# Logits ahead of transposes in two attentions, and one exponential moved behind a rounding copy

## What is computed

```python
def fox_prompt(q, k, v, logf):            # first attention, 8 heads x 64, causal
    s = jnp.einsum('bqhd,bshd->bhqs', qb, k).astype(jnp.float32) * scale
    s = s + cq[..., None] - ct[:, :, None, :]
    s = jnp.where(kpos[None, :] <= qpos[:, None], s, -jnp.inf)
    p = jax.nn.softmax(s, axis=-1).astype(v.dtype)
    return jnp.einsum('bhqs,bshd->bqhd', p, v)

def dsa_select_attend(...):               # second attention, 8 query heads on 2 key heads
    score = jnp.where(adm[None], score, -jnp.inf)
    _, idx = lax.top_k(score, top_k)      # the kernel adds a mask made of the scores instead
    return gathered_attention(q, k, v, idx, valid)
```

## Time and profile before

| | |
|---|---|
| median of 3 runs | 1360.31 us (1359.1 to 1361.63) |
| the profiled execution | 1360.25 us, span 1358.5 us |
| TensorE busy | 1317.5 us, 97% of the span |
| VectorE busy | 954.9 us, 70% |
| ScalarE busy | 676.5 us, 50% |
| first attention | about 296 to 427 us of the span |
| second attention | about 431 to 562 us of the span |

### The profile page before, as it was taken

The page is one execution under the profiler, slowest core; times in us unless marked ns, Lnnn a source line. Parts: engine busy times, 40 slices in busy tenths (PEclk is TensorE's granted clock), DMA queues, the critical chain, the costliest instruction groups (busy, mean ns, idle before and its releaser), DMA issues.

```text
span 1358.5 us, 23643 instructions
## 1 busy us (share of the span) xinstructions
PE 1317.5 (97%) x8868; PEld 1179.8 (87%) x8868; DVE 954.9 (70%) x1795; ACT 676.5 (50%) x1250; POOL 541.6 (40%) x518
## 2 busy tenths in 40 slices
PE   7989999989999999999999999999999999999997
PEld 7859999977877777778899999999999997678886
DVE  4399989898886989767855654555654556576497
ACT  5479979838885888510443222233223333343330
POOL 3406684532322132335645555555555452000011
PEclk9999999999999999999999999999999999999999
DMA  7102432259784622511045435445434459787452
GB/s 248 55 16 63 158 110 78 71 139 213 183 214 102 151 51 63 195 47 63 16 140 179 151 114 165 139 147 179 144 121 157 138 195 345 259 284 247 171 189 106
DMA packets 150369, 197.17 MB, mean 145 GB/s; under 512 B 28120, under 2 KB 106872, under 8 KB 150256
## 3 DMA queue, kind: packets, MB, share of 16 engines
q1 hardware_dynamic: 150256, 195.67, 46.6%
HBM read 136.69 MB, written 48.38 MB: 136 GB/s over the span
## 4 chain that ended last, share of the span: by engine, by line
PE 52%; DVE 3%; DMA 1%; issue 1%; ACT 1%; POOL 0%; POOLq 0%; SPq 0%; DVEq 0%; ACTq 0%
PE banks L2886 32%; PE banks L2258 6%; PE banks L2984 4%; PE banks L2985 4%; PE banks L2986 4%; DMA down_raw<-in_w_down 1%; DVE rows L3372 1%; DVE down_lo L3240 0%; PE banks L2860 0%; PE banks L3002 0%; DVE h_B_lo L3275 0%; DVE h_T_lo L3275 0%; PE banks L2356 0%; PE banks L2354 0%; ACT down_hi L3138 0%
## 5 line engine op out<-in xcount | busy, mean ns | idle before, releaser
L3160 POOL TENSOR_TENSOR w_lo<-w_S,w_hi 128x512 fp32r<-128x512 f32 x88 | 119.2, 1354 | 110.0 <-ACT w_hi L3039 110.0
L2886 PE MATMUL banks<-h_T_hi,w_hi 128*128 128x264 f32 x704 | 144.6, 285 | 0.2 <-DVE h_T_lo L3275 0.2
L2886 PE MATMUL banks<-h_T_lo,w_hi 128*128 128x264 f32 x704 | 143.7, 285 | 0.0
L2886 PE MATMUL banks<-h_T_hi,w_lo 128*128 128x264 f32 x704 | 142.9, 283 | 0.0
L3138 ACT CAST down_hi<-down_raw 128x1024 fp32r<-128x1024 f32 x77 | 80.7, 1051 | 123.8 <-PE banks L2986 62.1
L3039 ACT CAST w_hi<-w_S 128x512 fp32r<-128x512 f32 x88 | 54.7, 622 | 167.3 <-PE banks L2886 147.4
L2230 POOL TENSOR_TENSOR ln_rstd<-ln_var_eps,ln_power 128x1 f32<-128x1 f32 (+1 forms) x18 | 25.1, 1393 | 255.8 <-DVE ln_var_eps L2221 136.8
L3240 DVE TENSOR_TENSOR down_lo<-down_raw,down_hi 128x1024 fp32r<-128x1024 f32 x77 | 93.0, 1228 | 45.7 <-ACT down_hi L3138 45.5
L2984 PE MATMUL banks<-down_hi 128*128 128x512 f32 x308 | 121.0, 393 | 1.5 <-DVE rows L3372 1.1
L2986 PE MATMUL banks<-down_hi,down_lo 128*128 128x512 f32 x308 | 120.5, 391 | 0.0
L2985 PE MATMUL banks<-down_lo,down_hi 128*128 128x512 f32 x308 | 120.4, 391 | 0.0
(11 more groups left out here) (424 smaller groups left out, 3779.5 us busy)
## 6 DMA issues: line engine op xcount, KB each, us to landing
down_raw<-down_a SPq DMA_DIRECT2D x77, 256.0 KB, 4.0
gate_raw<-in_w_gate SPq DMA_DIRECT2D x11, 1024.0 KB, 6.5
down_t<-in_w_down SPq DMA_DIRECT2D x44, 256.0 KB, 4.1
down_w<-down_t SPq DMA_DIRECT2D x22, 512.0 KB, 3.4
down_raw<-in_w_down SPq DMA_DIRECT2D x22, 512.0 KB, 6.8
down_raw<-down_w SPq DMA_DIRECT2D x44, 256.0 KB, 4.3
up_raw<-in_w_up SPq DMA_DIRECT2D x10, 1024.0 KB, 6.3
down_a<-down_s SPq DMA_DIRECT2D x10, 1024.0 KB, 4.1
```

The lines of the kernel that those rows point to most:

```text
L2886: mm = nc.tensor.matmul(pp[:, bank[to] + ch, 0:PIECE], l, x[name][:, k, ch * PIECE:(ch + 1) * PIECE], start=opens and k == 0 and i == 0, s ...
L3160: nc.gpsimd.tensor_tensor(w_lo[n % 2][:, :, :], weight(m, SCHEME[q][0]), f32(w_hi[n % 2][:, :, :]), ALU.subtract).then_inc(w_lo_done, 1)
```

## The change

TensorE takes the first of a slot's logits ahead of the slot's transposes and the others behind them. This holds in both attentions, where the slot has a step and this is not one of a sample. The wait for banks and parts still stands ahead of both. Nothing is added or removed: the same instructions stand in another order.

On ScalarE, in the first attention alone (`own_first=True`), a slot with the first step of a batch now takes ahead of the rounding copy only those waiting exponentials that belong to that batch; the others come behind it.

```diff
--- before.py
+++ after.py
@@ -1321,7 +1321,7 @@
 def attention(nc, ctx, pl, exps, scales, c, tag, batches, parts_of_steps, ahead, source, loads, pe_first, act_first, dve_first, logits, bias,
               sample_values, sample_cols, places, out_sample, sp_beside=None, act_beside=None, pool_beside=None,
               dve_beside=None, pe_beside=None, pe_between=None, act_between=None, dve_between=None, spread=False, idle=(0, 0, 0), scales_soon=2 * NT,
-              sums_in_logits=False, pe_last=None, banks=None):
+              sums_in_logits=False, pe_last=None, banks=None, own_first=False):
 
 
 
@@ -1500,9 +1500,18 @@
             if max(wanted, default=0) > known:
                 known = max(wanted)
                 pe.wait_ge(freed, known)
+            ahead_of = slot.logits[:1] if slot.step and not slot.step.sample else []
+            for it in slot.logits:
+                if it not in ahead_of and slot.step:
+                    break
+                for o in it.after:
+                    if o.biased > known:
+                        known = o.biased
+                        pe.wait_ge(freed, known)
+                logits_of(it)
             if slot.step:
                 transposes(slot.step)
-            for it in slot.logits:
+            for it in slot.logits[len(ahead_of):] if slot.step else []:
                 for o in it.after:
                     if o.biased > known:
                         known = o.biased
@@ -1544,10 +1553,13 @@
                 act_between(act, it.n)
         waiting = []
         for slot in slots:
-            if slot.step is None or slot.step.firsts():
-                for it in waiting:
-                    exp(it)
-                waiting = []
+            firsts = slot.step.firsts() if slot.step else []
+            soon = max([i + 1 for i, it in enumerate(waiting) if it.batch in firsts], default=0)
+            if slot.step is None or firsts and not own_first:
+                soon = len(waiting)
+            for it in waiting[:soon]:
+                exp(it)
+            waiting = waiting[soon:]
             for batch in slot.joined:
                 if not batch.sample:
                     act.wait_ge(pv_done, batch.last.k + 1)
@@ -1947,7 +1959,7 @@
 
         attention(nc, ctx, pl, [[exp_a], [exp_b], [exp_c]], [scales], c, "fox", batches, filled(batches), fox_ahead(batches), source, loads, lambda pe: None,
                   lambda act: None, dve_first, logits, bias, sample_values, 4 * HD, places, out_sample, None, act_beside, None, dve_beside, pe_beside,
-                  pe_between, None, dve_between, spread=True, idle=(2, 0, 12))
+                  pe_between, None, dve_between, spread=True, idle=(2, 0, 12), own_first=True)
```

## The result

The changed kernel takes 1365.42 us (median of 5 runs, 1364.11 to 1367.61) against 1360.31 (1359.1 to 1361.63): a ratio of 1.0038, 95% interval 1.0027 to 1.0049. It is slower by 5.1 us, where +2.0 was forecast.

The account below looks back on a forecast made before the run. In a head TensorE, VectorE and ScalarE stand close together, so whichever comes late holds the others. Terms -3.6 + 2.9 + 0.4 - 0.3 + 0.5 + 1.1 + 1.0 = +2.0 gave 1362.2 us, range 1357.5 to 1365.7.

Parts of the forecast that it names:

- The copy ahead of the exponential, -3.6: First attention, head starts: rounding copy ahead of the 896-column exponential removes TensorE's 0.51 us wait in seven heads, -3.6 us.
- Slot 3's late copy, +2.9: First attention: the 1024-column product delays slot 3's copy 0.85 us; slot 7's transposes wait 0.42 us in seven heads, +2.9.
- The 6.43 us to the end of the exponential: First attention: after slot 3's start, the narrow exponential needed by slot 7's transposes ends at 357.40 us, not 356.55.
- The first head, +0.4: First attention's first head: transposes that filled time before the second narrow product now come behind it, +0.4 us.
- The second attention's start, -0.3: Second attention's start: a narrow product fills the 0.32 us gap where the first transposes wait for an exponential, -0.3 us.
- Slots 33 and 55, +0.5 and +1.1: Second attention: wide products ahead make copies 0.8 and 1.2 us late, delaying slots 35 and 59; +0.5 and +1.1 us.
- Slots 70 and 71, +1.0: Second attention's end: sample logits delay slot 70's copy 1.88 us; ScalarE's idle time returns 0.91, leaving +1.0 us.
- All other slots of the second attention, 0: Second attention, slots outside the start and those priced: no term in the sum, so no change in time.
- more late copies: Rival, second attention: ten more slots with wide products first; half costing 0.7 us adds 3.5, to 1365.7 us; chance 0.24.
- The forecast of no measurable change: Whole kernel: late copies in heads and three second-attention places, +2.0 us, within the 2.7 us counted as same; same had 0.47.
- third rival: Nothing changes: VectorE's order stays, so each wait removed on TensorE returns as a wait for it; 1360.3 us, chance 0.13.

Follow-up runs that it names:

- the fastest kernel: Changed kernel limited to the first attention, slot 3's 1024-column product left behind its transposes, head 5's stacking copies three half-heads later; 1356.74 us, ratio 0.9972.
- the profile of the first attention alone: Both TensorE's and ScalarE's order changed in the first attention, the second attention as in the kernel before; 1360.97 us, ratio 1.0000.
- the kernel with the second attention alone: Kernel before with only TensorE's new order, in the second attention, without `own_first=True`; 1367.99 us, ratio 1.0044.
- the kernel with the key-bias load ahead of head 4's copies: First-attention change without slot 3's product ahead; head 4's stacking copies moved behind the third head's key-bias load, head 5's two half-heads later; 1364.01 us.

## Why the prediction came out as it did

- **The copy ahead of the exponential, -3.6: right by itself, and smaller beside TensorE's part.** In the profile of ScalarE's part alone the four heads without a wait on key biases are 0.54 us shorter each, where 0.51 was forecast. In the fastest kernel, which has the narrow products ahead too, the six heads from the second on are 82.60 us together, against 86.19 before, and all seven are 3.3 us shorter, where -3.6 + 0.4 were predicted (its stage: 3.9). With slot 3's product ahead it is worth 0.3 a head. Alone it doesn't show in the time (-0.7, interval -2.4 to +1.1); that is open.
- **Slot 3's late copy, +2.9: the mechanism was right, the term too small in the heads.** The heads from the second on, without the third, are 13.77 us in the mean without that product ahead and 14.44 in the changed kernel: 0.67 us a head and not 0.42, and in the first head 13.77 against 12.65, 1.1. That is 6 x 0.67 + 1.1 = 5.1 us. The 6.43 us to the end of the exponential were good to 0.05, since the exponential's last row ends at 358.53, 6.48 us after the slot's start. What was missing is that TensorE starts 0.14 us after that end; together they make 0.61 us of lateness in this head. The timed runs with and without this product differ by 2.7 us, near the term. The profiles can't be compared over the stage, since the one without the product has 3.3 us of waits on key biases and the other none.
- **The first head, +0.4: right in size** with slot 3's product left out: 12.65 us against 12.32. It is regained in the second head, so it costs nothing, and the sum should not have had it.
- **The second attention's start, -0.3: the step failed.** It took an idle time of the weight loads for one of TensorE. The idle products fill it, and the product put there makes the first copy 0.4 us late.
- **Slots 33 and 55, +0.5 and +1.1:** measured 0.8 and 0.9. Right together, each off by 0.2 to 0.3.
- **Slots 70 and 71, +1.0:** measured 1.5. The 1.88 us of delay came as said, and ScalarE's idle time behind it gave 0.4 back and not 0.9.
- **All other slots of the second attention, 0: this step failed.** With the start they cost 2.9 us, so about 2.5 by themselves. The rival "more late copies" had the sign, and one of its sentences had the mechanism that slot 32 shows: transposes that covered a product's wait for its area now stand behind that wait. Its place was right only in part, since it named the wide products, and with narrow ones alone ahead 1.7 of the 2.9 us are there. Its price was 3.5. That its total came so near (1365.7 against 1365.42 measured) is luck: the 3.5 was 1.0 us too high, and the sum to which it was added had slots 33, 55, 70, 71 and the start 1.3 us too low together. What I had held against it, that VectorE is behind in those slots anyway, doesn't help: a product that waits for VectorE is just where the move hurts.

The sum of the terms as the traces size them is, for the second attention, 2.9 (the start and the other slots) + 0.8 + 0.9 + 1.5 = 6.1, of which the whole shows 5.2, so the places overlap by 0.9; for the first it is -3.9 + 5.1 = +1.2, and +1.8 in the profile of the first attention alone, where the timed runs say 0.0 [-1.4, +1.5]. The forecast of no measurable change fell because two terms of the second attention had been set at -0.3 and 0, where the runs show 2.9 together; the time stayed in the range because the range had been stretched to that rival's price.

The rule on the most-contended engine (the Trainium skill, Perfetto Trace Analysis, Identifying the Most-Contended Engine) names VectorE as the engine to work on first in a head. That no order of the others is worth anything was the prediction's reading of it, as its third rival. The fastest kernel leaves VectorE's order and its 12.50 us a head as they are, and its heads are 13.82 us long where they were 14.37:

```profile
353.40:367.22 13.82, 13.74 (x93) 11.07 (x91) 12.50 (x30) 12.14 (x28) 2.77 (x2) 1.00 0.75 184
```

TensorE is busy for 13.74 of them (columns as in the earlier trace rows). Here the measurement decides against that reading.

## What to carry to other kernels

Put an instruction that may wait ahead of one that can't only where its wait is over by then: the ready work that covered the wait now stands behind it, as in slot 32. Before counting a gap in the weight loads as free time, look whether TensorE itself is at work in it. And when a change does one good and one bad thing at several places, leave out the places one by one: in the first attention one slot in nine, taken out, turned no gain into 2.7 us.

## What the runs showed of the hardware

- One load of 512 KB, at the same place among the transfers, landed in 4.6 to 5.4 us in five profiles and in 6.6 to 8.1 in seven others, also where the first attention's program was the same. A third head with this wait is 1.5 to 2.4 us longer than that of a profile without it whose other heads are alike, by what looks like chance, and a single profile can't tell that from an effect of the edit.
- In the kernel with the second attention alone TensorE had waited 4.2 us at the barrier between the attentions, and the granted clock behind it was 0.50, the lower level of 1.2 GHz, in the first 4.91 us. The windows of that stretch (PE, PEld, DVE, ACT, POOL, clock, DMA):

```profile
430.09:435.09 5.00, 0.80 (x5) 0.36 (x3) 0.84 (x3) 0.00 (x0) 1.52 (x1) 0.92 0.14 39
435.09:440.00 4.91, 4.91 (x12) 3.62 (x12) 2.63 (x4) 1.25 (x2) 0.65 (x2) 0.50 0.38 107
```

  Its copies of the second attention were then 2.2 us late from the first slot on, where those of the other kernels with that order were 0.3 to 0.4 late: the wait of 4.2 us cost some 1.9 us more behind it, as the stage of 139.06 us says too. In the kernel with the key-bias load ahead of head 4's copies it was a wait of 3.7 us, a clock of 0.66 in the first 5 us, and 1.5 us more in the stage. After waits of up to 2.3 us at this barrier no such loss shows.
- The stop of 2.39 us among like products, in the kernel with ScalarE's part alone, stands at the same two products in the kernel with only narrow ones ahead, there for 1.02 us, and in no other profile of this case. Behind the longer one the granted clock was 0.65 in the 4.46 us of idle products; behind the shorter they took 3.02 us. What it waits for no run here shows.
